# Down projections of a SwiGLU trunk by Strassen's block algorithm, weight sums by accumulating DMAs

## The reference

```
def swiglu_ffn(h, w_gate_up, w_down):
    gu = h @ w_gate_up                      # (256, 2048) @ (2048, 11264)
    gate, up = gu[..., :D_FF], gu[..., D_FF:]
    return (jax.nn.silu(gate) * up) @ w_down   # (256, 5632) @ (5632, 2048)

for i in range(DEPTH):                      # DEPTH = 2
    h = rmsnorm(x, g[0]);  y = attention_i(h);  x = x + rmsnorm(y, g[1])
    h = rmsnorm(x, g[2]);  y = swiglu_ffn(h, ffn_w_gate_up[i], ffn_w_down[i])
    x = x + rmsnorm(y, g[3])
```

## Time and profile before

| | us |
|---|---|
| median of 3 runs | 2104.87 (2104.52 to 2105.41) |
| profiled execution, span | 2104.5 |
| TensorE (PE) busy | 2094.2 (100%) |
| VectorE (DVE) busy | 1615.4 (77%) |
| ScalarE (ACT) busy | 1152.9 (55%) |
| GpSimd (POOL) busy | 156.6 (7%) |
| DMA | 425.01 MB, mean 202 GB/s |

### The profile page before, as it was taken

How to read it: one execution, slowest core, us unless ns; L and a number is a source line. 1 busy time by engine, 2 the same in 40 slices (tenths; PEclk the granted TensorE clock), 3 DMA queues, 4 the chain that set the end, 5 groups by cost and what they waited for, 6 DMA issues and landing times.

```text
span 2104.5 us, 32177 instructions
## 1 busy us (share of the span) xinstructions
PE 2094.2 (100%) x9603; PEld 1718.9 (82%) x9603; DVE 1615.4 (77%) x3299; ACT 1152.9 (55%) x2061; POOL 156.6 (7%) x311
## 2 busy tenths in 40 slices
PE   9999999999999999999999999999999999999998
PEld 7877888888888888888888887888888888888886
DVE  6798677887667776678898898577877668776686
ACT  7666565544455454555666555665544545445553
POOL 2110000000000000000152343000000000000000
PEclk9999999999999999999999999999999999999999
DMA  7699866665666655665687787756555665556662
GB/s 257 211 247 253 223 206 206 195 191 173 199 199 199 197 171 190 199 204 161 202 247 219 214 251 215 234 190 216 189 187 178 199 217 184 188 178 203 206 193 87
DMA packets 221564, 425.01 MB, mean 202 GB/s; under 512 B 15808, under 2 KB 25440, under 8 KB 220976
## 3 DMA queue, kind: packets, MB, share of 16 engines
q1 hardware_dynamic: 214528, 402.45, 61.6%
q0 software_dynamic: 6672, 21.31, 3.7%
q10 hardware_dynamic: 288, 0.33, 0.1%
HBM read 409.31 MB, written 14.71 MB: 201 GB/s over the span
## 4 chain that ended last, share of the span: by engine, by line
PE 97%; DMA 1%; issue 1%; SPq 1%; ACT 0%; POOL 0%; DVE 0%; POOLq 0%
PE bank L1338 31%; PE bank L1340 31%; PE bank L1339 31%; PE bank L1385 1%; PE bank L1410 1%; PE bank L1351 1%; DMA x_sb<-x 0%; DMA p_f<-first_scratch 0%; DMA stage<-swa_w_out 0%; PE bank L1368 0%; SPq L541 0%; SPq L566 0%; PE bank L1432 0%; PE bank L1429 0%; PE bank L1571 0%
## 5 line engine op out<-in xcount | busy, mean ns | idle before, releaser
L1338 PE MATMUL bank<-ring_hi,a_hi 128*128 128x512 f32 x2240 | 880.3, 393 | 0.5 <-DVE ring_lo L817 0.5
L1340 PE MATMUL bank<-ring_hi,a_lo 128*128 128x512 f32 x2240 | 873.1, 390 | 0.0
L1339 PE MATMUL bank<-ring_lo,a_hi 128*128 128x512 f32 x2240 | 872.8, 390 | 0.0
L607 ACT ACTIVATE ring_hi<-stage,g_t 128x512 fp32r<-128x512 f32 x992 | 661.2, 717 | 376.6 <-DMA stage<-ffn_w_gate_up 203.0
L817 DVE SCALAR_TENSOR_TENSOR ring_lo<-stage,g_t,ring_hi 128x512 fp32r<-128x512 f32 x992 | 708.5, 759 | 147.3 <-ACT ring_hi L607 144.9
L1338 PEld LDWEIGHTS bank<-ring_hi,a_hi 128*128 128x128 f32 x2240 | 420.9, 188 | 92.9 <-issue 5.9
L1340 PEld LDWEIGHTS bank<-ring_hi,a_lo 128*128 128x128 f32 x2240 | 420.8, 188 | 88.1
L1339 PEld LDWEIGHTS bank<-ring_lo,a_hi 128*128 128x128 f32 x2240 | 421.1, 188 | 84.7
L815 DVE TENSOR_TENSOR ring_lo<-stage,ring_hi 128x512 fp32r<-128x512 f32 x480 | 305.5, 687 | 139.9 <-ACT ring_hi L605 138.5
L605 ACT ACTIVATE ring_hi<-stage 128x512 fp32r<-128x512 f32 x480 | 278.4, 624 | 225.0 <-PE bank L1340 149.5
L1338 PE MATMUL bank<-ring_hi,h_hi 128*128 128x512 f32 x704 | 274.6, 390 | 0.0
(11 more groups left out here) (148 smaller groups left out, 836.6 us busy)
## 6 DMA issues: line engine op xcount, KB each, us to landing
stage<-ffn_w_gate_up SPq DMA_DIRECT2D x352, 512.0 KB, 4.6
stage<-ffn_w_down SPq DMA_DIRECT2D x176, 512.0 KB, 5.5
stage<-fox_w_in SPq DMA_DIRECT2D x96, 512.0 KB, 4.7
stage<-swa_w_in SPq DMA_DIRECT2D x48, 512.0 KB, 4.7
stage<-swa_w_out SPq DMA_DIRECT2D x64, 256.0 KB, 6.2
stage<-fox_w_out SPq DMA_DIRECT2D x32, 512.0 KB, 5.5
first_scratch<-first_blocks SPq DMA_DIRECT2D x16, 384.0 KB, 5.4
p_f<-first_scratch SPq DMA_DIRECT2D x64, 96.0 KB, 3.9
```

What stands on the lines that cost most here:

```text
L607: nc.scalar.activation(ring_hi[:, n % RING, :], src, ACT.Identity, scale=g_t[:, row * KT + j:row * KT + j + 1]).then_inc(hi_ready, 1)
L1338: nc.tensor.matmul(dst, hi_a, hi_w, start=start, stop=False)
L1339: nc.tensor.matmul(dst, hi_a, lo_w, start=False, stop=False)
L1340: return nc.tensor.matmul(dst, lo_a, hi_w, start=False, stop=stop)
```

## The change

Groups 0 to 9 of each layer have no down unit any more. A SwiGLU block is 23 units: gate and up of group g for g = 0 to 10, and one plain down unit for group 10. The down projection of group g (g = 0 to 9) is computed by Strassen's algorithm (the form of Winograd) while gate and up of group g + 1 run: A is the hidden product (256 x 512), cut 2 x 2 into blocks of 128 tokens x 256; B is w_down's 512 x 1024 for two neighbouring blocks of output columns, cut 2 x 2 into 256 x 512. Such a "pair unit" does 7 block products of 2 `product` calls each, where the plain algorithm does 8. The gate unit of group g + 1 carries the seven for output columns 0 to 1023, the up unit those for 1024 to 2047. TensorE inserts them behind the steps of `PRODUCT_STEPS` (the seventh behind step 3 of the unit after), VectorE adds the banks to `y_sb` at `ADD_STEPS`, 7 additions for each pair unit, and ScalarE and VectorE split the weight blocks (each 128 x 1024, at `PAIR_HI`).

```
+NPROD = 7
+GW = FG - 1
+B11, B21, B22, T1, T2, T3, T4 = range(NPROD)
+PRODUCTS = (B11, B21, T1, T2, B22, T3, T4)
+BUFFER = {B11: 0, T1: 0, T2: 0, T4: 0, B22: 1, T3: 1, B21: 2}
+ADDED = {T1: (0, 1), T3: (0, 1), T2: (1, 1), T4: (1, 0)}
+PRODUCT_STEPS = ({18: 0, 20: 1, 22: 2, 24: 3, 26: 4, 29: 5}, {8: 0, 11: 1, 14: 2, 17: 3, 20: 4, 24: 5})
+LAST_PRODUCT, LAST_ADDED = 3, 5
+ADD_STEPS = ({20: 0, 22: 1, 24: 2, 26: 3, 28: 4, 31: 5}, {10: 0, 13: 1, 16: 2, 19: 3, 22: 4, 26: 5})
+PAIR_HI = ({5: (0, T1), 20: (0, T2), 22: (0, T3), 28: (0, T4), 24: (1, B11), 26: (1, B21), 31: (1, B22)},
+           {5: (0, T1), 13: (0, T2), 14: (0, T3), 22: (0, T4), 16: (1, B11), 19: (1, B21), 26: (1, B22)})
+HIDDEN_SPLIT = 14
+S_HI_STEPS = {17: 0, 19: 1}
+TURNED_STEPS = (0, 2)
```

**Weights.** SyncE loads three blocks for each pair unit (`load_down`, between its loads of gate and up tiles); the sums T1 to T4 are made in their place by accumulating DMAs from GpSimd's queue, each waiting until the value before it in the buffer was split:

```
+            def load_down(u, i):
...
+                for r, (k, c) in enumerate(((0, 0), (1, 1), (1, 0))):
+                    loaded = down_loaded[q % 2][r]
+                    if q % NP_LAYER < 2:
+                        sp.wait_ge(x_saved, 16 * (layer + 1))
+                    if q >= 2 and r == 0:
+                        sp.wait_ge(loaded, 16)
+                        sp.wait_ge(pair_lo, MADE[q - 2, T4] + 4 * NPROD * i)
...
+                    sp.dma_start(down_w[q % 2][r][:, :, :], rows.rearrange("(k p) n -> p k n", p=P)).then_inc(loaded, 16)
...
+            def sum_weights(q, k):
...
+                pool.wait_ge(pair_lo, MADE[q, {T1: B11, T3: B22, T2: T1, T4: T2}[k]])
...
+                pool.dma_start(to[:, :, :], w.rearrange("(k p) n -> p k n", p=P), accum_op=ALU.add).then_inc(sum_made[k], 16)
```

**The hidden product.** VectorE transposes it in 32 x 32 blocks with one instruction for each t (at steps 0 and 2 of the gate unit), GpSimd stores the blocks to DRAM and loads them back in their places, ScalarE and VectorE split all of it at steps 14 and 15, and four sums of blocks are made and split too:

```
+            def turn_group(u, i, t):
...
+                nc.vector.transpose(to, h_sb[:, t, :].rearrange("p (k b j) -> p b k j", b=4, j=Q)).then_inc(h_turned, 1)
...
+            def carry_hidden(f):
+
+                pool.wait_ge(h_turned, 2 * f + 2)
+                if f > 0:
+                    pool.wait_ge(h_loaded, 64 * f)
+                pool.dma_start(h_dram, h_blocks[:, :]).then_inc(h_stored, 16)
+                pool.wait_ge(h_stored, 16 * (f + 1))
+                if f > 0:
+                    pool.wait_ge(s_made, 4 * f)
+                    pool.wait_ge(ht_lo, f + 2 * (f // GW))
+                blocks = h_dram.rearrange("(a j) (b r) -> b j a r", j=Q, b=P // Q)
...
+                for b in range(P // Q):
+                    pool.dma_start(to[Q * b:Q * (b + 1)], blocks[b]).then_inc(h_loaded, 16)
...
+            def hidden_heads(u, i):
...
+                act.wait_ge(h_loaded, 32 * q + 64 + 128 * i)
...
+                nc.scalar.activation(h_hi[:, :, :].rearrange("p k (t a i) -> p (k t) a i", t=NT, i=Q), hidden_in(h_t), ACT.Identity).then_inc(ht_hi, 1)
...
+            def sum_hidden(u, i):
...
+                nc.vector.tensor_tensor(s_to[0], a21, a22, ALU.subtract).then_inc(s_made, 1)
+                nc.vector.tensor_tensor(s_to[3], a11, a21, ALU.subtract).then_inc(s_made, 1)
+                dve.wait_ge(s_made, made + 1)
+                nc.vector.tensor_tensor(s_to[1], s_to[0], a11, ALU.subtract).then_inc(s_made, 1)
+                dve.wait_ge(s_made, made + 3)
+                nc.vector.tensor_tensor(s_to[2], s_to[1], a12, ALU.add).then_inc(s_made, 1)
```

```
+            def down_pair(u, i, k):
...
+                if k == 0 and half == 0:
+                    pe.wait_ge(ht_lo, hidden_split(layer, g - 1, 0) + 2 * i)
+                if half == 0 and k in (2, 4):
+                    pe.wait_ge(s_lo_made, q + k // 2 + 4 * i)
+                pe.wait_ge(pair_lo, MADE[q, PRODUCTS[k]] + loop)
...
+                if added > 0:
+                    pe.wait_ge(pair_added, added + loop)
...
+                for r in range(2):
...
+                    last = product(ps[:, :], a_h, a_l, ring_hi[:, slot, :], ring_lo[:, slot, :], k < 3 and r == 0, r == 1, True)
+                last.then_inc(pair_done, 1)
```

**Room.** The buffers of weight blocks lie over `x_sb` and `g_b`. So x is saved to DRAM ahead of each SwiGLU block and loaded back at its end, and the gain row comes behind it:

```
                     if b == 2 * layer + 1:
                         pool.wait_ge(y_gained, 8 * b)
+                        save_x(b)
+                        for k in (T1, T3):
+                            sum_weights(NP_LAYER * layer, k)
+                        for g in range(GW):
+                            carry_hidden(GW * layer + g)
+                            q = NP_LAYER * layer + 2 * g
+                            for n, k in ((q, T2), (q, T4), (q + 1, T1), (q + 1, T3), (q + 1, T2), (q + 1, T4), (q + 2, T1), (q + 2, T3)):
+                                if n < NP_LAYER * (layer + 1):
+                                    sum_weights(n, k)
+                        load_x(layer)
                         load_gains(b + 1)
```

More of the change, by code:

```diff
@@ L132, with ffn_index, pair_unit, pair_number @@
 OUT_GAIN = {84: (0, 0), 88: (1, 0), 92: (0, 1), 98: (1, 1), 102: (0, 2), 106: (1, 2)}
-def step_order(s, first=False):
-    if first:
+def ffn_index(u):
+    for layer in range(2):
+        if U_FFN[layer] <= u < U_FFN[layer] + FFN_UNITS:
+            return layer, u - U_FFN[layer]
+    return None
+def pair_unit(u):
+    f = ffn_index(u)
+    return f is not None and 2 <= f[1] < 2 * FG
+def pair_number(u):
+    layer, n = ffn_index(u)
+    return NP_LAYER * layer + n - 2
+def in_fours(u):
+    f = ffn_index(u)
+    return f is not None and 1 <= f[1] < 2 * FG - 1
@@ new lines, in tiles_rested @@
+def tiles_rested(u, s):
+    f = ffn_index(u)
+    uneven = f is not None and f[1] > 0
+    before = ffn_index(u - 1) if u else None
+    uneven_before = before is not None and 0 < before[1] < 2 * FG
+    if s == 0:
+        if u == 0:
+            return []
+        return tiles_rounded(u - 1, STEPS - 1) if uneven_before else [(u, UT - 1)]
+    if uneven and f[1] < 2 * FG:
+        return tiles_rounded(u, s - 1)
+    if uneven and s == 1:
+        return [(u, 15)]
+    return [(u + 1, s // 2 - 1)] if s % 2 == 0 else []
@@ new lines, in pairs_rounded, with ring_places @@
+def pairs_rounded(u, s):
+    f = ffn_index(u)
+    if f is None or f[1] == 0 or s not in PAIR_HI[f[1] % 2]:
+        return []
+    later, k = PAIR_HI[f[1] % 2][s]
+    return [(u + later, k)] if pair_unit(u + later) else []
+def ring_places():
+    place, before, last = {}, {}, {}
+    n = 0
+    for u in range(U_END):
+        f = ffn_index(u)
+        fixed = f is not None and f[1] >= 2
+        if fixed and f[1] == 2:
+            first = n % RING
+        for j in range(UT):
+            slot = (first + j) % RING if fixed else n % RING
+            if not fixed:
+                n += 1
+            place[u, j] = slot
+            before[u, j] = last.get(slot)
+            last[slot] = ("tile", u * UT + j)
+        if pair_unit(u):
+            for k in range(NPROD):
+                p = NPROD * pair_number(u) + k
+                done = NPROD * pair_number(u) + PRODUCTS.index(k)
+                slot = (first + UT + 2 * (p % 4)) % RING
+                place["pair", p] = slot
+                before["pair", p] = last[slot + 1]
+                last[slot] = last[slot + 1] = ("pair", done)
+        if fixed and f[1] == 2 * FG:
+            n = first + UT
+    return place, before
@@ L365, in half, with per_loop, looped @@
             return slice(first, first + CH // 2)
+        def per_loop(u):
+            return UT * (FFN_LOOP_UNITS if ffn_index(u) else LOOP_UNITS)
         def whole_program(loop, unit):
[L369 removed]
+            def looped(u, n, units=LOOP_UNITS):
                 with loop(n) as i:
[L371 removed]
+                    for part in range(units):
                         unit(u + part, i)
```

347 lines of the change are left out of this document (266 added, 81 removed).

## The result

| | before | after |
|---|---|---|
| median of the runs, us | 2105.14 (2104.52 to 2105.8) | 2301.86 (2298.11 to 2303.23) |
| ratio, 95% interval | | 1.0931 [1.0916, 1.0947] |
| profiled span, us | 2104.5 | 2299.5 |

What follows compares the result with a forecast made beforehand. TensorE was taken to bound the kernel, each product removed being worth 0.68 us. 2104.5 - 54.4 + 14 (hidden product's way) + 6 (ends of the block) = 2070 us, with a range of 2051 to 2150.

Steps and rivals of the forecast that it cites:

- TensorE's 54.4 us: 28 products for a down unit's 32 save 2.72 us a group, 10 groups, 2 layers: -54.4 us.
- VectorE and ScalarE: VectorE gains 3.9 us a group (84% busy), ScalarE some 5 us; both hidden under TensorE, costed at nothing.
- The way of the hidden product: Store to DRAM and strips back in each gate unit: stall of 0.7 us a group, +14 us; upper end 8.6 a group.
- last strip: Landing of the last of four strips of the hidden product loaded back: 3.9 us; 5.8 as the median of all.
- The start: VectorE multiplies and turns t = 1 of the hidden product, done at T0 + 2.0 us from the gate unit's start.
- The store: GpSimd's 512 KB store of the hidden product: 4.6 us, from 384 KB landing in 3.9 us as a median.
- rival 2: Store and strips slow, last strip landing in 7.3 us: stall of 3.7 us a group, 2130 us; chance 0.10.
- the clock: Pauses long enough to drop TensorE's granted clock to its lower level would add to rivals 1 or 2; no size given.
- T2: Weight sum in an up unit, 7.4 us for its accumulating DMA: taken as 6 us, no stall; upper end 3.1 a group.
- The ends: Save and load of x and load of `g_b` at SwiGLU block ends: 3 us a layer, between 0 and 8; +6 us.
- Rival 1: Accumulating DMAs make the DMA engines the bound: 65.2 us a group if bytes count twice, 2107 to 2225 us; chance 0.25.

Runs made afterwards that it cites:

- e9_gains_late: Changed kernel with the hidden product turned on TensorE, T2 asked for later, x loaded early, gain row and last quarter of x late: 2089.0 us, ratio 0.9927.
- e3_neither: Changed kernel with the hidden product stored and loaded only in each layer's first group, and plain loads for the accumulations: 2110.93 us.
- e1_no_carry: Changed kernel with the hidden product stored and loaded only in each layer's first group, stale values elsewhere: 2151.64 us.
- e12_order_only: Changed kernel, way through DRAM kept, with T2 to T4 later in the up unit, x loaded early and gains late: 2253.03 us.
- e10_blocks_late: Changed kernel with one constant changed, so SyncE issues an up unit's three weight blocks one pair of tiles later: 2318.21 us, ratio 1.1019.
- e2_plain_sums: Changed kernel with the accumulating DMAs of the weight sums replaced by plain loads of the same size: 2267.72 us.
- e5_later_t2: As `e4_pe_turned`, all accumulations kept, but TensorE asks for T2 three steps later in the up units: 2102.76 us, ratio 0.9982.
- e8_pe_plain: As `e4_pe_turned`, with plain loads in place of the accumulations: 2103.58 us.
- e4_pe_turned: Changed kernel with the hidden product turned by eight TensorE transposes and copied by ScalarE, without store, strips or VectorE transposes: 2146.64 us, ratio 1.0192.

## Why the prediction was wrong, step by step

**TensorE's 54.4 us: right.** The three large lines have 2240 + 304 + 320 matmuls each, 8592 in all, and a group without waits takes 62.56 us and the transposes.

**VectorE and ScalarE: right.** The block of 1024 has a record of 1218 ns against a pitch of 1.14 taken, ScalarE's 1056 ns against 0.9 to 1.1; VectorE was at 82% (`e9_gains_late`) and 85% (`e3_neither`) in the loop for the 84% of the forecast.

**The way of the hidden product: the step that failed.** Taken at +14 us, it cost 150 us in 18 groups (`e1_no_carry`) and 182 in 20 (`e12_order_only`, against `e9_gains_late`). The sum was T0 + 2.0 + 4.6 + 1.7 + 3.9 + 2.4 = T0 + 14.6, against a need at T0 + 14.3. In the group above T0 is 614.5 us, the start of the gate unit's first matmul:

| term | forecast | measured | 
|---|---|---|
| t = 1 turned, store issued | 2.0 | 618.36 - 614.5 = 3.9 |
| store of 512 KB | 4.6 | 7.25 (median 7.3) |
| issues of the strips | 1.7 | 1.68 and 0.3 ahead |
| last strip | 3.9 | 4.34 |
| splits | 2.4 | 634.50 - 631.92 = 2.6 |
| sum | 14.6 | 20.0 |

Two terms make 4.5 of the 5.4 us. *The start*: my 2.0 leave at most 0.6 us ahead of VectorE's two instructions for t = 1; they began at 616.57, T0 + 2.1, behind the rests that stand in front in its list. *The store*: I scaled a store measured under other traffic by its bytes. Here the three blocks are issued 0.9 us before it, and the engines are at 1.06. The row that fits was there: 7.3 us, the longest of 16 stores. I wrote down this collision in rival 2 and set against it that SyncE's queue is another one; that was no shield, for the store fell to 5.9 us where the same blocks came behind it (`e10_blocks_late`). The Trainium skill's fit of 2.0 us and the bytes' rate (DMA: Bandwidth & Descriptors, Anatomy of one DMA) gave 3.2 us for the store, and the measurement of 7.3 decides against it under this load. My own upper end for the stall, 8.6 us a group, held the 5.5; the range, at 2150, left it out.

Then **the clock**, which I named in one clause and priced at nothing. A pause of 5.5 us is followed by matmuls at 0.43 us instead of 0.23, at a granted clock of 0.50, from 634.50 to 638.81: ten matmuls in 4.3 us for 2.3. With what follows T2's pause the group loses 2.5 us in this way. That makes 7.5 to 8.0 us a group for the way, for 150/18 = 8.3 measured by taking it out. Of the 62 us that TensorE was busy for longer, 50 are gone in `e3_neither` (2101.8 - 2052.0, for the same matmuls).

**T2: mis-sized.** I took 6 us for an accumulation against a budget of 7.4; it lands in 6.9 as a median, but T2's of the up unit in 9.1 to 9.8 where the trace of the changed kernel was read. It cost 34 us (`e2_plain_sums`) to 44 (`e5_later_t2`). The upper end of 3.1 us a group (62 us) held it.

**The ends: mis-sized.** Forecast 3 us for each layer. In `e8_pe_plain`, which has neither the way nor the doubled bytes, 2101.9 - 2050.1 - 18 for the transposes = 34 us are left, 17 a layer: 18.5 us of waits for `h_sb` at the last down unit, some smaller ones, and the clock behind them. The 59 us of `e3_neither` are more because its first groups still make the way: their 22.6 us of waits belong to that step. (In the first group of the changed kernel the store lands in 8.2 us, and the last strip in 7.3.) I had added the load of x and `g_b` to the first gain's time, but not to that of the last down unit's tiles, which is where they decided.

**The rivals.** Rival 2 named the mechanism (`h_lo`, ScalarE waiting for `h_t`), at a strip of 7.3 us and a chance of 0.10; it was the store and the start instead, and the 3.7 us a group became over 8. Rival 1 had the price of the byte right: 0.87 x 72.31 = 62.9 us of DMA work in a group for 65.2 forecast. Its conclusion, that the engines then set the time, was not borne out: `e9_gains_late`, with 57.7 us of DMA work, has them at 0.91 with TensorE at 100%. There the accumulations hurt by when they land, not by how much they are. (Two slips in its sum: a group of 65.2 us gives 2109 with the ends and not 2107, and a range up to 2150 takes in the lowest third of 2109 to 2225, not the lower half.) My range added such costs as alternatives, of which one would occur; three occurred at once, in series, and none hid another.

## What to carry to other kernels

A chain of dependent transfers must be summed from its worst landings in the stretch where it will run, with everything issued there on any queue, and its start taken from the place in the list of the engine that feeds it. A pause of TensorE costs more than it lasts, for the clock behind it: here 5.5 us cost 7.5 to 8. And before data go out to DRAM and back to be turned, price the transposes on the engine that waits for them: 0.9 us a group did here what the detour did for 9.1.

## What the runs showed of the hardware that I had not expected

- An accumulating DMA from DRAM into SBUF costs the engines 1.9 times a plain one's time for each byte (5.95 against 3.17 us for each MB, `e1_no_carry` and `e3_neither`); GpSimd needs 1.2 us to issue it (changed kernel), for 0.72 of the same load without the sum (`e2_plain_sums`).
- TensorE's clock fell to the lower level (granted 0.50) even behind a pause of 1.84 us in `e4_pe_turned` (ahead of 694.08), and stayed there for 3.4 us of dense matmuls, from 694.65 us on. After the pause of 1.66 us ahead of 673.07 in the changed kernel the matmuls were back at a pitch of 0.23 us after two. What tells the two apart stays open.
- DMA engines at a mean share of 0.91 and 248 GB/s still let TensorE run a whole group without any wait (`e9_gains_late`), once T2 had three steps more than its 7.4 us, some 9.4, to land in.
